# Branch b's tiles by 512- and 256-column matmuls, and another order of conditioning tiles, in a two-block transformer kernel

## What is computed

```
mod = silu(c) @ w_ada + b_ada            # 6 vectors of 2048: sh1 sc1 g1 sh2 sc2 g2
h   = x * (1 + sc1) + sh1
z_u, z_v, z_h, z_g = split(h @ w_in + b_in)
y_a = spatial_gating(gelu(z_u), gelu(z_v), ...) @ w_branch_a     # [256,1024] @ [1024,2048]
y_b = hyena(z_h, ...) @ w_branch_b                               # [256,1024] @ [1024,2048]
gate_a, gate_b = split(sigmoid(z_g))
mix = (gate_a * y_a + gate_b * y_b) @ w_o + b_o
x   = layer_norm(alpha * x + g1 * mix, ln1_g, ln1_b)
h   = x * (1 + sc2) + sh2
f   = square(relu(h @ w_m1 + b_m1)) @ w_m2 + b_m2
x   = layer_norm(alpha * x + g2 * f, ln2_g, ln2_b)
```

## Time and profile before

| | |
|---|---|
| median of 3 runs | 2395.21 us (2394.74 to 2397.94) |
| profiled execution | 2395.05 us, span 2393.3 us |
| mean granted clock of TensorE | 0.997 |
| PE busy | 2361.5 us, 99% of the span |
| DVE busy | 1725.3 us, 72% |
| ACT busy | 1062.4 us, 44% |
| HBM | 233 GB/s over the span |

### The profile page before, as it was taken

How to read it: one execution, slowest core, us unless ns; L and a number is a source line. 1 busy time by engine, 2 the same in 40 slices (tenths; PEclk the granted TensorE clock), 3 DMA queues, 4 the chain that set the end, 5 groups by cost and what they waited for, 6 DMA issues and landing times.

```text
span 2393.3 us, 30201 instructions
## 1 busy us (share of the span) xinstructions
PE 2361.5 (99%) x12960; PEld 2017.5 (84%) x12960; DVE 1725.3 (72%) x1608; ACT 1062.4 (44%) x1032; POOL 29.9 (1%) x61
## 2 busy tenths in 40 slices
PE   7999999999999999999999999999999999999998
PEld 6888888888788888888888888987888888888886
DVE  7877678878777777776787666898764666764675
ACT  5564544434334334465554444434533443443433
POOL 0000000000000000000000000000000000000000
PEclk9999999999999999999999999999999999999999
DMA  7343477877777777766645448776555567765552
GB/s 276 140 141 143 185 258 279 292 267 264 282 290 285 283 294 271 298 242 228 264 173 187 177 179 300 296 292 237 193 192 193 194 225 279 289 262 193 194 193 106
DMA packets 79813, 558.68 MB, mean 233 GB/s; under 512 B 9034, under 2 KB 11285, under 8 KB 13248
## 3 DMA queue, kind: packets, MB, share of 16 engines
q1 hardware_dynamic: 74832, 528.25, 59.2%
q0 software_dynamic: 4848, 28.50, 3.3%
HBM read 547.26 MB, written 9.45 MB: 233 GB/s over the span
## 4 chain that ended last, share of the span: by engine, by line
PE 96%; DVE 2%; DMA 1%; ACT 1%; issue 0%; SPq 0%; ACTq 0%; DVEq 0%
PE ps L627 34%; PE ps L630 16%; PE ps L714 11%; PE ps L716 11%; PE ps L715 11%; PE ps L625 1%; PE ps L595 1%; PE ps L596 1%; PE ps L597 1%; DMA stage<-wstream 1%; DVE w_lo L1617 1%; PE ps L650 1%; PE ps L652 1%; PE ps L651 1%; PE ps L1054 1%; PE ps L1044 1%
## 5 line engine op out<-in xcount | busy, mean ns | idle before, releaser
L1617 DVE TENSOR_TENSOR w_lo<-stage,w_hi 128x2048 fp32r<-128x2048 f32 x400 | 915.0, 2289 | 433.7 <-ACT w_hi L1127 428.8
L1127 ACT ACTIVATE w_hi<-stage 128x2048 fp32r<-128x2048 f32 x400 | 764.2, 1911 | 785.1 <-DMA stage<-wstream 483.6
L627 PE MATMUL ps<-xs,w_hi 128*128 128x512 f32 x3136 | 973.5, 396 | 0.0
L630 PEld LDWEIGHTS ps<-xs,w_lo 128*128 128x128 f32 x2936 | 551.5, 188 | 129.8
L630 PE MATMUL ps<-xs,w_lo 128*128 128x256 f32 x2936 | 578.1, 278 | 0.0
L627 PEld LDWEIGHTS ps<-xs,w_hi 128*128 128x128 f32 x3136 | 485.6, 189 | 11.4 <-issue 3.1
L714 PE MATMUL ps<-w_hi,hs 128*128 128x512 f32 x976 | 381.4, 391 | 0.0
L716 PE MATMUL ps<-w_lo,hs 128*128 128x512 f32 x976 | 379.8, 389 | 0.0
L715 PE MATMUL ps<-w_hi,hs 128*128 128x512 f32 x976 | 379.8, 389 | 0.0
L1939 DVE SCALAR_TENSOR_TENSOR stage<-stage,cond 128x2048 f32<-128x2048 f32 x96 | 219.4, 2285 | 3.4 <-DMA stage<-wstream 3.3
L714 PEld LDWEIGHTS ps<-w_hi,hs 128*128 128x128 f32 x976 | 183.2, 188 | 40.2 <-issue 2.1
(11 more groups left out here) (441 smaller groups left out, 2188.3 us busy)
## 6 DMA issues: line engine op xcount, KB each, us to landing
stage<-wstream SPq DMA_DIRECT2D x497, 1024.0 KB, 4.8
spectra<-k_made POOLq DMA_DIRECT2D x4, 1024.0 KB, 6.6
k_spec<-spectra POOLq DMA_DIRECT2D x4, 1024.0 KB, 6.1
xraw<-xT SPq DMA_DIRECT2D x4, 512.0 KB, 11.6
resid<-x SPq DMA_DIRECT2D x2, 1024.0 KB, 15.1
w<-w POOLq DMA_DIRECT2D x16, 128.0 KB, 6.6
parked<-resid POOLq DMA_DIRECT2D x1, 2048.0 KB, 10.6
resid<-parked POOLq DMA_DIRECT2D x1, 2048.0 KB, 8.2
```

Source lines behind the costliest of these rows:

```text
L627: mm = pe.matmul(out[c], hi[c], rhs[:, k, :], start=(first and j == 0), stop=end)
L630: mm = pe.matmul(out[c][:, S:2 * S], lo[c], rhs[:, k, 0:S], start=False, stop=False)
L1127: act.activation(high(w)[:, 0:m], stage[:, n % RING, 0:m], ACT.Copy).then_inc(hi_ready, 1)
L1617: tt(w_lo[:, slot, 0:m], stage[:, slot, 0:m], f(high(w)[:, 0:m]), ALU.subtract).then_inc(lo_ready, 1)
```

## The change

- The tiles of `w_branch_b` become `whole`: 16 matmuls of 512 and 16 of 256 columns per tile in place of 48 of 256. ACT copies the cross half of each to `tev`; DVE adds the main half, then multiplies by `gate_b`, then adds `mixacc`: three operations of 128 x 512 in place of two.
- Five conditioning tiles are taken out of `COND_LATE` (steps 238, 240, 242, 264, 266) and five more are put in the first MLP; there the steps 83, 84, 86, 87, 88, 90, 91, 92, 94 stand where 84, 86, 88, 90, 92, 94 stood, and 115, 116, 118, 119, 120, 122 where 116, 118, 120, 122 stood. The conditioning vector's return to its buffer (`cond_moved`) is waited for ahead of step 242, not 238.
- In `w_o`, DVE makes the splits of tiles 272 and 273 in step 269, ahead of that step's eviction.
- In `into_stage` for `ln1`, `part_lo(name, 1)` is moved ahead of `gate_step(1, 1, ...)`.

```
-COND_MLP1 = (*range(2, 25, 2), 26, ..., 62, *range(64, 123, 2))
+COND_MLP1 = (*range(2, 25, 2), 26, ..., 62, *range(64, 84, 2), 83, 84, 86, 87, 88, 90, 91, 92, 94, *range(96, 115, 2), 115, 116, 118, 119, 120, 122)
-COND_LATE = tuple(range(T_BA - 4, T_WO + 10, 2))
+COND_LATE = tuple(range(T_BA + 2, T_WO + 6, 2))
...
-    if T_BA <= w < T_BB:
+    if T_BA <= w < T_WO:
         return "whole", U_BA + w - T_BA, 0
-    if T_BB <= w < T_WO:
-        return "half", U_BA + w - T_BA, 0
...
@@ ACT, branch b @@
         for w in range(T_BB, T_WO):
             split(w + 2)
             if w > T_BB:
                 mix_hi(U_BB + w - T_BB - 1)
+            take_cross(job(w)[1], w, tev)
...
@@ DVE, into_stage @@
             part_lo(name, 0)
+            part_lo(name, 1)
             if name == "ln1":
                 gate_step(1, 1, g1_row)
-                part_lo(name, 1)
...
@@ DVE, w_in and branch a @@
-            if w == T_BA - 4:
-                dve.wait_ge(sem("cond_moved"), 32)
-            if w - T_Z in COND_Z or w >= T_BA - 4:
+            if w - T_Z in COND_Z:
                 condition(w + 2)
...
+        dve.wait_ge(sem("cond_moved"), 32)
         for w in range(T_BA, T_BB):
...
@@ DVE, branch b, after split, condition and mix_lo(u - 2) @@
-            summed(dve, u, w)
             t = tev[:, u % 2]
-            dve.wait_ge(evac_done, u - 1)
+            dve.wait_ge(cross_ready, cross_count(u) + 1)
             c = 2 * (u - U_BB)
-            took(tt(t, acc(u), gate_b[:, c:c + 2, :], ALU.mult), u)
+            took(tt(t, acc(u), t, ALU.add), u)
+            link(tt(t, t, gate_b[:, c:c + 2, :], ALU.mult))
             tt(t, t, mixacc[:, c:c + 2, :], ALU.add).then_inc(sem("mix_ready"), 1)
...
@@ DVE, w_o @@
         for w in range(T_WO, T_MLP2):
-            if w < T_MLP2 - 1:
+            if w < T_WO + 12 or w == T_MLP2 - 2:
                 split(w + 2)
                 condition(w + 2)
...
             if w == T_WO + 11:
                 residual_bias(3)
+                split(T_MLP2 - 2)
+                split(T_MLP2 - 1)
```

More of the change, by code:

```diff
@@ L82 @@
 N_ADA = 96
-COND_MLP1 = (*range(2, 25, 2), 26, 28, 32, 34, 36, 38, 40, 44, 46, 48, 50, 52, 54, 56, 58, 60, 62, *range(64, 123, 2))
+COND_MLP1 = (*range(2, 25, 2), 26, 28, 32, 34, 36, 38, 40, 44, 46, 48, 50, 52, 54, 56, 58, 60, 62, *range(64, 84, 2), 83, 84, 86, 87, 88, 90, 91, 92, 94, *range(96, 115, 2), 115, 116, 118, 119, 120, 122)
 COND_Z = (4, 6, 14, 18, 20, 22)
-COND_LATE = tuple(range(T_BA - 4, T_WO + 10, 2))
+COND_LATE = tuple(range(T_BA + 2, T_WO + 6, 2))
 COND_STEPS = (*(T_MLP1 + a for a in COND_MLP1), *(T_Z + a for a in COND_Z), *COND_LATE)
@@ L163, in begins @@
     kind, u, k0 = job(w)
-    return kind in ("whole", "half", "pair", "narrow") or k0 == 0 or T_WOUT <= w < T_MLP1 and k0 == 8
+    return kind in ("whole", "pair", "narrow") or k0 == 0 or T_WOUT <= w < T_MLP1 and k0 == 8
 def ends(w):
@@ L173, in ends @@
         return k0 in (4, 12)
-    return kind in ("whole", "half", "pair", "narrow") or k0 == (12 if kind == "tok" else 8)
+    return kind in ("whole", "pair", "narrow") or k0 == (12 if kind == "tok" else 8)
 def columns_of(w):
@@ L194, in cross_count @@
         return u - U_IN
-    if U_Z <= u < U_BB:
+    if U_Z <= u < U_WO:
         return N_CROSS_IN + 4 * UPU + u - U_Z
-    return N_CROSS_IN + up_count(u) + (U_BB - U_Z if u >= U_BB else 0)
+    return N_CROSS_IN + up_count(u) + (U_WO - U_Z if u >= U_WO else 0)
 COLS = {}
@@ L738, in tile @@
                 mm = narrow(w, rhs, u)
-            elif kind in ("up", "cross", "whole"):
+            else:
                 mm = both_halves(w, rhs, k0, 8, u, first, ends(w), ready, hook)
[L741 to L747, removed]
             mm.then_inc(tile_done, 1)
```

5 lines of the change are left out of this document (2 added, 3 removed).

## The result

The changed kernel takes 2402.3 us (median of 9 runs, 2401.76 to 2404.39), the kernel before 2395.21 in the runs beside it: a ratio of 1.003, 95% interval 1.0021 to 1.0038. That is 7.1 us more, where the sum in the prediction has 6.5. The profiled execution's own time is 2402.55 us, its span 2400.7 against 2393.3.

The account below looks back on a forecast made before the run. TensorE (PE) was taken as the bound, 96% of the chain that ended last. The terms +4.3 + 5.8 - 0.5 - 2.5 - 0.6 = +6.5 us on 2395.05 gave 2401.5 us, range 2395.0 to 2405.5.

Parts of the forecast that it names:

- Branch b: Branch b's eight tiles: DVE becomes the bound, 13.45 us per two tiles against 11.2 on PE; +4.3 us.
- The walk from 1538.50: Branch b's evictions counted on from tile 250's: 252 at 1550.60, 254 at 1564.05, 256 at 1577.50; `T_WO` starts at 1578.3.
- The rival by which DVE is not the bound: Branch b: the copy is hidden and DVE had slack, PE's 1.6 us count; +0.6 in all, 2395.7 us, chance 0.12.
- The ring: First MLP: at tiles 87, 91, 95, 119, 123 the weight tile is issued second of a pair and PE waits; +5.8 us.
- four short waits and one long: First MLP: of five PE waits of 0.9 or 2.2 us, four short and one long taken, within 4.5 to 11 us.
- the rival: First MLP: the ring order does no harm; +0.7 in all, 2395.8 us, chance 0.15.
- Ahead of branch a: PE wait ahead of 1488.23, from a weight tile queued late in the ring, goes with the dropped conditioning; -0.5 us.
- Last tiles: End of `w_o`: splits of 272 and 273 ahead of tile 269's eviction remove PE's waits; -2.5 us, or -1.5.
- seam: Seam into the second MLP: `part_lo` of part 1 leaves the chain of the second token half; -0.6 us.
- the 1 us that the prediction left in the range: Seam, 1670 to 1675, granted clock 0.81: 1 us can come or go with the shifted waits.
- The sum: Whole kernel: +4.3 + 5.8 - 0.5 - 2.5 - 0.6 = +6.5 us.
- the rival that the clock falls in the new waits: Waits ahead of `T_WO` and in the MLP lower PE's clock, 1 to 2 us each: +3, 2404.5 us, chance 0.07.

Follow-up runs that it names:

- branch_only: The kernel before with branch b's edit alone (whole tiles, ACT's copy, third DVE operation): 2399.71 us, ratio 1.0018.
- clean_deal: The changed kernel with as many conditioning steps in the first MLP, but never three of their loads among five in a row: 2398.83 us, ratio 1.0014.
- seam_both: The kernel before with the splits of tiles 272 and 273 ahead of the eviction and `part_lo(name, 1)` ahead of `gate_step(1, 1, ...)`: 2393.52 us, ratio 0.9992.
- splits_only: The kernel before with only the splits of tiles 272 and 273 moved ahead of the eviction: 2394.53 us, ratio 0.9996.
- deal_only: The kernel before with only the change's two new lists of conditioning steps: 2399.69 us, ratio 1.0016.
- clean_lo: The changed kernel with never three conditioning loads among five in the first MLP, and branch b's `mix_lo` ahead of split and conditioning: 2394.59 us, ratio 0.9998.
- tail_deal: The changed kernel with two of three first-MLP steps conditioning from 64 to 93, every second from 94 to 122: 2402.21 us, ratio 1.003.
- lo_first: The changed kernel with branch b's `mix_lo` moved on DVE ahead of the split and the conditioning step: 2400.52 us, ratio 1.002.
- tail_lo_two: The changed kernel with first-MLP conditioning densest at steps 64 to 93, branch b's `mix_lo` first, two of its four conditioning steps moved out: 2395.75 us, ratio 1.0004.

## Why the prediction was right, step by step

- **Branch b**, forecast +4.3: +4.6 in the trace of after, +4.4 and a median of +4.3 alone. The walk from 1538.50 holds row by row: a DVE pair of 13.45 us was forecast and 13.55 is there; PE waits of 0.4, 0.9, 2.3 and 2.3 us ahead of tiles 252, 254, 256 and 258 were forecast, and 0.35, 0.74 and 2.06 are listed. The fourth shows as 0.53, since PE came late to it (below), and as 2.02 in `branch_only`. DVE's wait for the copy is 0.72 us, not 0.66. The rival by which DVE is not the bound is out. The eviction forecast to start the pair, 1550.60, is at 1558.15, which less the 7.52 us lost by the eviction of tile 250 (1546.02 against 1538.50) is 1550.63.
- **The ring**, forecast +5.8, four short waits and one long: the short ones 0.63 to 0.92 us and the long one 2.21, at the five tiles named and at none other in that stretch, summing to 5.2 us in the list and 6.6 by the starts of the tiles, as PE also runs empty at each. `clean_deal` shows that the order does it, so the rival is out. That one of five would be long was a choice between 4.5 and 11 us on the word of two pairs, and it came out with some luck. Which pair would be the long one was not forecast; it is the fourth (issued at 981.25, the weight tile there at 990.01, 8.8 us later), and why that landing is late stays open.
- **Ahead of branch a**, forecast -0.5: -0.5. The size is that of two executions: in the four kernels that keep conditioning steps 238 to 242 that wait is 0.31 (before), 0.79 (`branch_only`), 1.39 (`seam_both`) and none (`splits_only`), and in the ten that drop them it never shows.
- **Last tiles**, forecast -2.5, **and seam**, -0.6: together -3.0 from `w_o` to the seam's last wait, as forecast, and another -1.1 behind it, which is the clock (below). Right in sum and sign, but the reason for the first was wrong. The prediction gives the -2.5 to the two splits ahead of the eviction; alone they bring 0.8 (1.1 by the trace), and the dropped conditioning steps 264 and 266, which it only mentions as absorbing DVE's lag, remove that wait without them (`deal_only`, -2.4 to the seam). The step that failed is "PE stands before tile 272, whose split DVE makes only after the eviction": DVE was 3.4 us behind for another reason. The term's size came out because the change does both, so that part of it is luck. `part_lo`, forecast 0.6, brought 0.4 and 0.6 by the two pairs of traces that tell.
- **The clock.** The seam, which the earlier trace rows show at 0.81, lies 9 us later in after, and there the clock is 1.00 (first row below). That is the 1 us that the prediction left in the range. It comes and goes. Of the fourteen traces five have a fall in or just behind PE's last wait in the seam (before, `splits_only`, `seam_both`, `clean_lo`, `tail_deal`), and from that wait to the first 24-matmul tile they take 88.9 to 89.2 us; the nine without it take 88.0. The wait itself is 1.26 or 1.27 us in all of them.
- **The sum.** The stages of the trace named above have +4.6 + 6.6 - 0.5 - 3.0 = +7.7, where the prediction has +6.5: the ring is short by 0.8 and branch b by 0.3. The two profiled executions differ by 7.5 all the same, since the +1.1 that after had lost ahead of the change and the -1.1 of the seam's clock, neither of them due to the change, cancel in this pair. The medians have +7.1.

```profile
1679.00:1684.00 5.00, 3.30 (x25) 1.00 0.58 198
...
1573.00:1579.00 6.00, 6.00 (x28) 0.72 0.28 117
```

Both rows are of after. The second stands behind its wait of 2.06 us in branch b, so the rival that the clock falls in the new waits saw the fall rightly, but not its price. There it cost nothing, since DVE was the bound: from 1572.54 to `w_o` are 13.51 us, and 13.51 in `branch_only` (1566.28 to 1579.79), where the clock stays at 1.00. What the clock took came out of the next wait, 0.53 in place of 2.02 us. The Trainium skill ("TensorE: Matmul & The Clock Gate", section "The HAM clock gate") has the throttled state as the default that activity releases; the falls behind waits agree, but of ten PE waits of 2.0 to 2.2 us in these traces only four were followed by a fall (994 us in `deal_only` and `lo_first`, 1572.54 in after, 1566.81 in `clean_deal`).

## What to carry to other kernels

In a ring of buffers, moving one load changes which others are issued together. Count, for every load after the moved one, how many are ahead of it in its group and when it is needed; room on the engine that uses it is not enough. Nor is idle time of VectorE a sign that a step can go there: what stands behind it in the queue, and who waits for that, decides (`tail_lo_two`). When an operation waits for another engine's product, put the wait's cause one large operation earlier in the queue, as `lo_first` did, before judging the form that brought the wait: with that and two steps moved out, 512-column matmuls that had cost 4.3 us earned the 1.6 us that they save PE.

## What the hardware showed that I had not expected

- A wait of 2 us can cost nearly twice its length: behind 2.02 us at 994.12 (`deal_only`) the granted clock was 0.67 and 0.76 in two stretches of 3 us, 1.8 us lost. The clock also falls at the wait of 1.27 us in the seam in five of fourteen traces, for 0.9 to 1.1 us. It didn't happen behind the same wait of after (2.21 us, clock 1.00). So a repair elsewhere may look smaller or larger by that much; `lo_first` gave 1.8 us by its median and 4.1 in its branch b, though no trace shows how often the clock fell in its runs.
- Two loads of 1 MB issued together are there after 4.8 and 7.5 us in one place and the second after 8.8 us in another (801.62 and 981.25 of after), a single one after 4.9 (801.09 of `clean_deal`).
- An operation of 0.60 us on ACT leaves DVE idle for 0.72 and stretches the distance between its neighbours from 0.6 to 1.41 us.
